# Last expert's result rows placed by a product on TensorE, the other rows gathered during that expert, and its up projection in two halves

## The chip, the core and the metric

The kernel runs on one core of a Trainium2 chip. The metric is the device time of one execution in microseconds (us), median of three runs. TensorE is called PE below, VectorE is DVE, ScalarE is ACT, GpSimd is POOL and SyncE is SP.

## What is computed

A two-layer decoder trunk on 512 tokens of 1024 values. Each layer adds a mixer's output to x, then the output of a mixture of 16 experts, of which every token uses two. The part that matters here is the second one, of both layers:

```
combine = jnp.einsum('tk,tke->te', top_w, jax.nn.one_hot(eid, N_EXPERTS)) * pg[:, None]
out = jnp.zeros_like(t)
for e in range(N_EXPERTS):
    y = (jax.nn.silu(t @ w_gate[e]) * (t @ w_up[e])) @ w_down[e]
    out = out + combine[:, e:e + 1] * y
```

Weights are float32: `w_gate[e]` and `w_up[e]` are 1024x512, `w_down[e]` is 512x1024. Behind layer 0 stands layer 1's norm and a convolution mixer, behind layer 1 the final norm.

## The kernel before

**Experts.** Only the tokens that picked an expert are computed, up to 96 (`CAP`) of them; a branch that these inputs do not take handles more. POOL gathers an expert's token rows from HBM (L557, into `xg`), PE turns them (L1887), ACT and DVE make a high and a low part of the turned rows (`xgT`), and each product is three matmuls of such parts (`mm3`, L1558 to L1560). Weights stream through a ring in SBUF (SP, L304), and ACT and DVE split them too, chunk by chunk of 128x1024: ACT casts the high part (L605), DVE subtracts for the low part (L911). The split ring has six chunks, so chunk c is split only when PE is done with chunk c-6 (`chunk_done`). One expert is 12 chunks: 4 gate, 4 up, 4 down.

**Order.** It is written out by hand. In step e PE does gate(e), turns the hidden rows of e-1 (L1911), up(e), turns the token rows of e+1, and down(e-1), 24 matmuls for each of the three projections. ACT does silu (L788), DVE the product silu*up (`hidden`, L1384, into `act_h`), both the copies of turned rows (ACT L793, DVE L1377) and of the result y (ACT columns 0 to 511, L801; DVE the rest, L1391), which ACT's queue then stores to HBM (L806). Steps 5 to 14 run in a loop; the last step has gate(15), turn, up(15), down(14), then alone turn of hidden(15) and down(15).

**Tail of a layer.** In `result_rows` DVE works out the weights of a token's two experts and the HBM rows of its two results (22 small instructions, L1338 to L1356), behind down(14). POOL waits until all 16 results are stored, and gathers them by tokens in eight DMAs of 128 rows (L572, two for each of four tiles of 128 tokens, into `y_back`). DVE adds them to x with their weights (`combine`, L1329, two instructions a tile). Then comes the norm: sum of squares on ACT (L648), root on POOL (L490, L493), scaling on DVE (L932). Behind layer 0 PE turns the tiles (L1540), ACT and DVE copy them (L639, L939), and PE starts the odd layer's projection in `first_piece`, for 256 tokens, when tiles 0 and 1 are copied. Behind layer 1 the scaled tiles are stored as the output (SP, L366).

## Time and profile before

| | us |
|---|---|
| median of three runs | 1208.0 (1206.04 to 1209.63) |
| the profiled execution, its own time | 1209.83 |
| its span in the trace | 1207.9 |
| PE busy | 1097.2 (91%) |
| DVE busy | 887.1 (73%) |
| ACT busy | 645.2 (53%) |
| POOL busy | 121.7 (10%) |

The span is the time from the first to the last recorded instruction. Busy shares are averages over stages; idle time on an engine counts only where the chain of waits goes through it. The granted clock is the share of 2.4 GHz that PE had; 0.5 is 1.2 GHz.

### The profile page before, as it was taken

The page shows a single profiled execution, that of the slowest core. Times are in us where ns is not written, and L with a number is a line of the kernel's source. Part 1 is how long each engine was busy: PE and PEld are TensorE (multiplying, and loading weights), DVE is VectorE, ACT ScalarE, POOL GpSimd, SP SyncE. Part 2 cuts the span into 40 slices and gives each one's busy share as a digit, 9 for nine tenths or more (in the row PEclk, how much of TensorE's full clock was granted, in tenths as well). Part 3 has the DMA queues.
Part 4 walks back from the last instruction along what each step waited for, and adds up shares of the span by engine and source line. Part 5 has one row for each costly group of instructions (what it writes and reads, how often), then busy time and mean ns, then how long its engine had stood idle before and what let it go on. Part 6 is the DMA issues. An engine that isn't in the chain of part 4 may idle for free.

```text
span 1207.9 us, 15260 instructions
## 1 busy us (share of the span) xinstructions
PE 1097.2 (91%) x5316; PEld 831.7 (69%) x5316; DVE 887.1 (73%) x1125; ACT 645.2 (53%) x799; POOL 121.7 (10%) x158
## 2 busy tenths in 40 slices
PE   5999999789899999999983899999999999999980
PEld 4776776567777777777762888778877777777750
DVE  5253555867788999999994462553688999999975
ACT  5133434421347888888871321232267888888841
POOL 2000000021211000000004100000111000000005
PEclk9998999889979999999996899999879999999995
DMA  8632222220259999999974633233169999999935
GB/s 302 189 125 70 79 79 70 70 88 13 75 190 356 378 408 396 397 397 411 410 283 158 255 106 104 70 105 105 71 224 359 402 391 396 410 397 396 418 123 208
DMA packets 77598, 286.35 MB, mean 237 GB/s; under 512 B 16647, under 2 KB 16647, under 8 KB 61164
## 3 DMA queue, kind: packets, MB, share of 16 engines
q1 hardware_dynamic: 65212, 241.64, 52.6%
q0 software_dynamic: 8608, 30.95, 7.9%
q10 hardware_dynamic: 3728, 13.11, 2.8%
q8 instruction: 30, 0.49, 0.2%
q14 instruction: 20, 0.16, 0.0%
HBM read 266.79 MB, written 20.20 MB: 238 GB/s over the span
## 4 chain that ended last, share of the span: by engine, by line
PE 83%; DVE 9%; ACT 2%; DMA 2%; issue 2%; POOL 1%; ACTq 0%; POOLq 0%; SPq 0%; DVEq 0%; PEldq 0%
PE ps L1558 25%; PE ps L1560 25%; PE ps L1559 24%; PE ps L1887 2%; DVE w_split L911 2%; PE ps L1540 1%; ACT w_split L605 1%; PE ps L1803 1%; DVE arena L1277 1%; DMA arena<-y_rows_dram,arena 1%; PE ps L1645 1%; DVE arena L932 1%; DVE x_sb L1329 1%; PE ps L1911 1%; DVE arena L1105 1%
## 5 line engine op out<-in xcount | busy, mean ns | idle before, releaser
L911 DVE TENSOR_TENSOR w_split<-ring,w_split 128x1024 fp32r<-128x1024 f32 x452 | 540.9, 1220 | 87.5 <-ACT w_split L605 75.4
L605 ACT CAST w_split<-ring 128x1024 fp32r<-128x1024 f32 x452 | 472.2, 1051 | 195.1 <-PE ps L1560 191.5
L1558 PE MATMUL ps<-w_split,hT 128*96 128x512 f32 (+1 forms) x960 | 391.4, 408 | 14.2 <-DVE hT L1377 6.2
L1560 PE MATMUL ps<-w_split,hT 128*96 128x512 f32 (+1 forms) x960 | 383.8, 400 | 0.0
L1559 PE MATMUL ps<-w_split,hT 128*96 128x512 f32 (+1 forms) x960 | 383.6, 400 | 0.0
L1558 PEld LDWEIGHTS ps<-w_split,hT 128*96 128x96 f32 (+1 forms) x960 | 165.0, 172 | 79.3 <-issue 11.6
L1560 PEld LDWEIGHTS ps<-w_split,hT 128*96 128x96 f32 (+1 forms) x960 | 164.1, 171 | 63.4
L1559 PEld LDWEIGHTS ps<-w_split,hT 128*96 128x96 f32 (+1 forms) x960 | 165.4, 172 | 57.5 <-issue 0.3
L1558 PE MATMUL ps<-hT,w_split 128*128 128x512 f32 (+1 forms) x384 | 147.5, 384 | 5.7 <-issue 4.1
L1559 PE MATMUL ps<-hT,w_split 128*128 128x512 f32 (+1 forms) x384 | 145.0, 378 | 0.0
L1560 PE MATMUL ps<-hT,w_split 128*128 128x512 f32 (+1 forms) x384 | 144.8, 377 | 0.0
L1558 PEld LDWEIGHTS ps<-hT,w_split 128*128 128x128 f32 x384 | 73.9, 193 | 26.6 <-issue 11.5
L557 POOL DMA_INDIRECT arena<-h_rows_dram,arena x30 | 42.3, 1410 | 435.4 <-PE ps L1887 356.4
L1560 PEld LDWEIGHTS ps<-hT,w_split 128*128 128x128 f32 x384 | 74.0, 193 | 13.3
L1559 PEld LDWEIGHTS ps<-hT,w_split 128*128 128x128 f32 x384 | 74.1, 193 | 12.3
L648 ACT ACTIVATE arena<-x_sb 128x1024 f32<-128x1024 f32 x20 | 21.2, 1058 | 84.1 <-DVE x_sb L1190 40.9
L490 POOL TENSOR_SCALAR st<-st 128x1 f32<-128x1 f32 (+1 forms) x28 | 15.5, 553 | 373.5 <-ACT arena L648 229.1
L1540 PE MATMUL ps<-ident,arena 128*128 128x128 f32 x128 | 20.8, 316 | 31.0 <-DVE arena L932 30.3
L932 DVE SCALAR_TENSOR_TENSOR arena<-x_sb,st,arena 128x1024 f32<-128x1024 f32 x20 | 31.8, 1588 | 23.1 <-POOL st L493 23.1
L702 ACT ACTIVATE x_sb<-x_sb,st 128x128 f32<-128x128 f32 (+3 forms) x32 | 17.8, 556 | 43.8 <-DVE st L1043 43.8
L1540 PEld LDWEIGHTS ps<-ident,arena 128*128 128x128 f32 x128 | 17.2, 164 | 34.3 <-DVE arena L932 22.8
L1038 DVE SCALAR_TENSOR_TENSOR x_sb<-ps,arena 128x256 f32<-128x256 f32 (+3 forms) x16 | 13.2, 823 | 37.4 <-PE ps L1645 37.4
(218 smaller groups left out, 846.4 us busy)
## 6 DMA issues: line engine op xcount, KB each, us to landing
ring<-in_exp_w_gate SPq DMA_DIRECT2D x64, 1024.0 KB, 10.5
ring<-in_exp_w_up SPq DMA_DIRECT2D x64, 1024.0 KB, 10.7
ring<-in_exp_w_down SPq DMA_DIRECT2D x64, 1024.0 KB, 11.7
ring<-in_w_in_even SPq DMA_DIRECT2D x14, 1024.0 KB, 10.1
y_rows_dram<-arena ACTq DMA_DIRECT2D x32, 384.0 KB, 6.9
ring<-in_w_in_odd SPq DMA_DIRECT2D x12, 1024.0 KB, 7.3
ring<-in_w_out_even SPq DMA_DIRECT2D x4, 1024.0 KB, 4.8
h_rows_dram<-arena POOLq DMA_DIRECT2D x8, 512.0 KB, 4.5
```

Of the source, the lines that this page charges most:

```text
L490: g.tensor_scalar(dst, src, 1.0 / width, EPS, ALU.mult, ALU.add).then_inc(pool_step, 1)
L557: g.indirect_dma_start(out=xg[0:CAP, e % 2, :], out_offset=None, in_=h_dram, in_offset=bass.IndirectOffsetOnAxis(ap=slot_tok[0:CAP, e:e + ...
L605: s.copy(hi_of(c), raw(c)).then_inc(hi_ready, 1)
L648: s.activation(junk, x_sb[:, t, :], ACT.Square, accum_out=st[:, t:t + 1]).then_inc(sumsq_ready, 1)
L702: s.activation(e_maps[:, u % 2, m, 0:n], e_maps[:, u % 2, m, 0:n], ACT.Exp, bias=st[:, 16 + c:17 + c], accum_out=st[:, 20 + c:21 + c]).the ...
L911: v.tensor_tensor(lo_of(c), raw(c), hi_of(c).bitcast(F32), ALU.subtract).then_inc(lo_ready, 1)
L932: ins = v.scalar_tensor_tensor(out=h_row, in0=row, scalar=st[:, 4 + t:5 + t], in1=gains, op0=ALU.mult, op1=ALU.mult)
L1540: last = nc.tensor.transpose(ps[:, turn_bank(n, t) + b, k * P:(k + 1) * P], h_rows[:, t, c * P:(c + 1) * P], ident[:, :])
L1558: mm(out, a[0], b[0], start=start, stop=False)
L1559: mm(out, a[1], b[0], start=False, stop=False)
L1560: return mm(out, a[0], b[1], start=False, stop=stop)
L1887: last = nc.tensor.transpose(ps[:, 5 + k // 4, (k % 4) * P:(k % 4) * P + CAP], xg[0:CAP, u, k * P:(k + 1) * P], ident[0:CAP, 0:CAP])
```

## The change

It changes both layers in the same way, from expert 13 on.

- **Order of the last expert.** The hidden rows of expert 14 are turned in the middle of down(13), and down(14) comes before gate(15), in PSUM banks 5 and 6. SP loads the weights in that order. y of 13, 14 and 15 is copied by ACT alone, in two copies each.
- **Halves.** up(15) is made as two products of 256 columns (24 matmuls each); the hidden rows of the first half are made and turned while the second is computed, and down(15) starts with them.
- **Gather.** POOL no longer waits for the store of expert 15; it gathers when experts 0 to 14 are stored. A token whose result is in expert 15's row gets the row of its other expert instead, with weight 0 in `combine`.
- **Product.** Four small fp16 products turn the last expert's 0/1 selection to `selT`; when y of 15 is in SBUF, eight plain float32 products of 128x512 (`last_rows`, K=96) put its rows at their tokens in all eight PSUM banks, and `add_last` adds them to x with weight `last_w`, one DVE instruction a tile.
- **Small work.** The row numbers (`result_rows`, now 16 instructions) are worked out before gate(15)'s splits; the weights (`result_weights`, 8 instructions) within down(15). The constants get an `ident16` (one memset and one select on POOL at the start). Two more steps (13, 14) are written out instead of looped.
- **Behind layer 0** DVE splits three of the four first chunks of the odd weights behind the adds.

The core of the diff:

```diff
@@ gpsimd, take_back
-                    for u in range(2):
-                        pool.wait_ge(y_stored[u], 16 * (E // 2) * (l + 1))
+                    pool.wait_ge(y_stored[0], 16 * (E // 2) * (l + 1))
+                    pool.wait_ge(y_stored[1], 16 * ((E // 2) * (l + 1) - 1))
+                    pool.wait_ge(last_sel_ready, l + 1)
@@ scalar, after step 14
+            def last_experts(l, n, c):
+                copy_last_y(1, 2, c, 16 * ((n - 2) // 2))
+                store_y(E - 3, n - 2, 1)
+                splits(c + 9)
+                copy_last_y(0, 5, c + 4, 16 * ((n - 1) // 2))
+                store_y(E - 2, n - 1, 0)
+                act.wait_ge(last_sel_turned, l + 1)
+                s.copy(selT[0:CAP, :, :], ps[0:CAP, 7, :].rearrange("p (t n) -> p t n", t=TT)).then_inc(last_sel_ready, 1)
+                splits(c + 13)
+                silu(n, c + 8)
+                splits(c + 14)
+                copy_last_actT(l, n, 0)
+                splits(c + 16)
+                copy_last_actT(l, n, 1)
+                splits(c + 18)
+                copy_last_y(1, 2, c + 16, 16 * (n // 2))
+                store_y(E - 1, n, 1)
@@ vector, after step 14
                 result_rows(l)
+                splits(c + 14)
+                last_hidden(l, n, c, 0)
+                splits(c + 15)
+                copy_last_actT(l, n, 0)
+                splits(c + 16)
+                last_hidden(l, n, c, 1)
+                result_weights(l)
+                copy_last_actT(l, n, 1)
@@ vector, behind layer 0
             experts(0)
-            splits(PIECE * (ODD_BASE + 1))
             combine(0, 0)
             combine(0, 1)
+            splits(PIECE * ODD_BASE + 1)
+            add_last(0, 0, x_ready)
+            add_last(0, 1, x_ready)
+            add_last(0, 2, x_freed)
             scaled(2, 0)
+            add_last(0, 3, x_freed)
             scaled(2, 1)
             low_part(2, 0)
-            combine(0, 2)
+            splits(PIECE * ODD_BASE + 4)
             low_part(2, 1)
-            combine(0, 3)
+            combine(0, 2, x_ready)
+            combine(0, 3, x_ready)
@@ tensor, after step 14
+            def last_expert(l, n, c):
+                down(n - 1, 0, c, None, bank=5)
+                ... (four products of sel and ident16)
+                gate(n, 1, c + 4, None)
+                for half in range(2):
+                    for k in range(KD):
+                        if half and k == KD // 2:
+                            pe.wait_ge(half_act, l + 1)
+                            turn_half(n, 0)
+                        last = mm3(ps[0:CAP, (1, 7)[half], 0:256], ..., slice(half * 256, half * 256 + 256), ...)
+                pe.wait_ge(half_actT, l + 1)
+                down_rows(1, c + 12, None, 0, 2)
+                pe.wait_ge(act_ready, n + 1)
+                turn_half(n, 1)
+                down_rows(1, c + 12, None, 1, 2)
+                pe.wait_ge(actT_ready, n + 1)
+                down_rows(1, c + 12, None, 2, 2)
+                down_rows(1, c + 12, None, 3, 2)
+            def last_rows(l):
+                for t in range(TT):
+                    for half in range(2):
+                        last = mm(ps[:, 2 * t + half, :], selT[0:CAP, t, :].bitcast(F32), y_sb[0:CAP, 1, half * 512:half * 512 + 512], ...)
+                    last.then_inc(last_full, 1)
```

DVE in the last expert of layer 1. Before, from the product silu*up of 15 to the row numbers:

```order
L1384 TENSOR_TENSOR arena<-arena,ps 96x512 [waits chunk_done,silu_ready]
L911 TENSOR_TENSOR w_split<-ring,w_split 128x1024 [waits hi_ready] x2
L1391 COPY arena<-ps 96x512 [waits y_stored0,chunk_done]
L1377 TENSOR_TENSOR hT<-ps,hT 128x4x96 [waits actT_hi]
L1338 TENSOR_REDUCE arena<-arena 128x4 [waits route_exp]
```

Now, from the end of the row numbers on (L1473 is the half product, L1483 the low part of turned hidden rows, L964 a weight chunk's low part):

```order
L1421 CAST arena<-arena 128x8 [waits dve_step]
L964 TENSOR_TENSOR w_split<-ring,w_split 128x1024 [waits hi_ready] x8
L1473 TENSOR_TENSOR arena<-arena,ps 96x256 [waits up_half,silu_ready]
L964 TENSOR_TENSOR w_split<-ring,w_split 128x1024 [waits hi_ready]
L1483 TENSOR_TENSOR hT<-ps,hT 128x2x96 [waits half_hi]
L964 TENSOR_TENSOR w_split<-ring,w_split 128x1024 [waits hi_ready]
L1473 TENSOR_TENSOR arena<-arena,ps 96x256 [waits chunk_done,silu_ready]
```

The row numbers now stand in front of eight splits, and a split stands in front of each half's low part.

ACT in the last expert of layer 1, before, from the last split but one to the store of 15 (L801 is half of y, L806 the store):

```order
L605 CAST w_split<-ring 128x1024 [waits chunk_done,slot_landed3] x2
L801 COPY arena<-ps 96x512 [waits y_stored0,chunk_done]
L806 DMA y_rows_dram<-arena 96x1024 [waits y_dve,y_act]
L793 CAST hT<-ps 128x4x96 [waits act_turned]
L801 COPY arena<-ps 96x512 [waits y_stored1,chunk_done]
L806 DMA y_rows_dram<-arena 96x1024 [waits y_dve,y_act]
```

Now, from the last split in front of y of 14 to the first half's turned rows (L824 and L825 are the halves of y, L860 the store, L846 `selT`, L834 half of the turned hidden rows):

```order
L622 CAST w_split<-ring 128x1024 [waits chunk_done,slot_landed0]
L824 COPY arena<-ps 96x512 [waits y_stored0,chunk_done]
L825 COPY arena<-ps 96x512
L860 DMA y_rows_dram<-arena 96x1024 [waits y_half1,y_half0]
L846 CAST hT<-ps 96x512 [waits last_sel_turned]
L622 CAST w_split<-ring 128x1024 [waits chunk_done,slot_landed0]
L622 CAST w_split<-ring 128x1024 [waits chunk_done,slot_landed1] x2
L622 CAST w_split<-ring 128x1024 [waits chunk_done,slot_landed2]
L805 ACTIVATE arena<-ps 96x512 [waits act_ready,chunk_done]
L622 CAST w_split<-ring 128x1024 [waits chunk_done,slot_landed2]
L834 CAST hT<-ps 128x2x96 [waits half_turned]
```

The store of 14 has moved in front of the silu of 15 and of the splits for up(15) and down(15); the turned rows of a half stand where those of the whole stood.

DVE behind layer 1's experts, before:

```order
L1329 SCALAR_TENSOR_TENSOR x_sb<-arena,x_sb 128x1024 [waits y_back_loaded0]
L1329 SCALAR_TENSOR_TENSOR x_sb<-arena,x_sb 128x1024 [waits dve_step]
L1329 SCALAR_TENSOR_TENSOR x_sb<-arena,x_sb 128x1024 [waits y_back_loaded1]
L1329 SCALAR_TENSOR_TENSOR x_sb<-arena,x_sb 128x1024 [waits dve_step]
L932 SCALAR_TENSOR_TENSOR arena<-x_sb,st,arena 128x1024 [waits norm_rstd,gain_loaded]
```

Now (L1393 is `combine`, L1381 `add_last`, L985 the scaling):

```order
L1393 SCALAR_TENSOR_TENSOR x_sb<-arena,x_sb 128x1024 [waits y_back_loaded0]
L1393 SCALAR_TENSOR_TENSOR x_sb<-arena,x_sb 128x1024 [waits dve_step]
L1393 SCALAR_TENSOR_TENSOR x_sb<-arena,x_sb 128x1024 [waits y_back_loaded1,dve_step]
L1393 SCALAR_TENSOR_TENSOR x_sb<-arena,x_sb 128x1024 [waits dve_step]
L1381 SCALAR_TENSOR_TENSOR x_sb<-ps,arena,x_sb 128x1024 [waits last_full,dve_step]
L1393 SCALAR_TENSOR_TENSOR x_sb<-arena,x_sb 128x1024 [waits y_back_loaded2]
L1393 SCALAR_TENSOR_TENSOR x_sb<-arena,x_sb 128x1024 [waits dve_step]
L1381 SCALAR_TENSOR_TENSOR x_sb<-ps,arena,x_sb 128x1024 [waits last_full,dve_step]
L985 SCALAR_TENSOR_TENSOR arena<-x_sb,st,arena 128x1024 [waits norm_rstd,gain_loaded]
```

Each tile has a third instruction, which waits for PE's product instead of for a DMA.

## Rows read from the trace of the kernel before

**Rows 1.** Waits: engine, line waited for, us in total, times, longest

```profile
POOL arena L572 <- DMA y_rows_dram<-arena: 75.9, 2, 39.3
PE ps L1540 <- DVE arena L932: 30.3, 4, 20.1
DVE x_sb L1329 <- DMA arena<-y_rows_dram,arena: 19.1, 4, 11.2
```

**Rows 2.** Windows: us, busy (instructions) by engine, clock, DMA share, GB/s

```profile
1136.40:1153.90 17.50, 17.50 (x85) 12.51 (x84) 16.65 (x17) 14.34 (x17) 0.57 (x1) 1.00 1.02 415
1173.80:1207.90 34.10, 0.00 (x0) 0.00 (x0) 15.84 (x13) 5.15 (x9) 16.04 (x16) 0.56 0.54 196
632.80:641.40 8.60, 8.52 (x24) 5.43 (x24) 4.36 (x23) 0.05 (x1) 0.00 (x0) 0.65 0.07 23
641.40:661.40 20.00, 0.00 (x0) 0.00 (x0) 9.47 (x8) 4.82 (x7) 11.92 (x11) 0.61 0.66 229
```

**Rows 3.** Chain of waits behind layer 1's down(15): start, us, what

```profile
1171.66 0.23 PE ps L1558
...
1173.83 0.70 DVE arena L1391
1174.60 3.70 DMA y_rows_dram<-arena
1178.34 0.75 issue
...
1180.38 5.33 DMA arena<-y_rows_dram,arena
1185.73 1.30 DVE x_sb L1329
...
1201.98 1.28 DVE arena L932
```

**Rows 4.** Timeline of layer 0's tail: start, us, engine, line, instruction, idle before

```profile
653.61 2.61 DVE L1329 SCALAR_TENSOR_TENSOR x_sb<-arena,x_sb 128x1024 f32<-128x1024 f32 x2 [6.62 <-DMA arena<-y_rows_dram,arena]
...
660.09 1.29 DVE L932 SCALAR_TENSOR_TENSOR arena<-x_sb,st,arena 128x1024 f32<-128x1024 f32 x1 [0.54 <-POOL st L493]
...
668.14 1.22 DVE L939 TENSOR_TENSOR hT<-ps,hT 128x1024 fp32r<-128x1024 f32 x1
...
669.46 0.55 PE L1558 MATMUL ps<-hT,w_split 128*128 128x256 f32 x1 [4.05 <-issue]
```

**Rows 5.** Timeline, DVE: product silu*up of three experts; splits, low parts

```profile
625.02 0.68 DVE L1384 TENSOR_TENSOR arena<-arena,ps 96x512 f32<-96x512 f32 x1
...
1143.25 0.68 DVE L1384 TENSOR_TENSOR arena<-arena,ps 96x512 f32<-96x512 f32 x1
1143.85 0.95 DVE L1370 TENSOR_TENSOR hT<-ps,hT 128x768 fp32r<-128x768 f32 x1
1144.71 4.81 DVE L911 TENSOR_TENSOR w_split<-ring,w_split 128x1024 fp32r<-128x1024 f32 x4
...
1160.88 0.68 DVE L1384 TENSOR_TENSOR arena<-arena,ps 96x512 f32<-96x512 f32 x1
```

**Rows 6.** Timeline of layer 1's last expert: ACT's casts, PE, copies, small instructions

```profile
1158.39 0.39 PE L1558 MATMUL ps<-w_split,hT 128*96 128x512 f32 x1
...
1164.12 0.58 ACT L801 COPY arena<-ps 96x512 f32<-96x512 f32 x1 [1.66 <-PE ps L1560]
...
1166.25 0.16 DVE L1338 TENSOR_REDUCE arena<-arena 128x4 f32<-128x16 f32 x1
1166.39 0.47 PE L1558 MATMUL ps<-w_split,hT 128*96 128x512 f32 x1 [1.98 <-DVE hT L1377]
...
1168.25 0.63 PE L1559 MATMUL ps<-w_split,hT 128*96 128x512 f32 x1
...
1171.31 0.17 DVE L1356 CAST arena<-arena 128x8 int32<-128x8 f32 x1
```

**Rows 7.** POOL's gathers: timeline of two of experts, one of L572; L557's durations

```profile
430.32 0.92 POOL L557 DMA_INDIRECT arena<-h_rows_dram,arena  x1 [16.66 <-PE ps L1887]
448.39 1.70 POOL L557 DMA_INDIRECT arena<-h_rows_dram,arena  x1 [17.15 <-PE ps L1887]
1181.63 0.94 POOL L572 DMA_INDIRECT arena<-y_rows_dram,arena  x1 [0.30 <-issue]
L557 POOL DMA_INDIRECT arena<-h_rows_dram,arena x30: 907/914/4657, 347.8 to 1106.8; - x30
```

**Rows 8.** PE: float32 products of 1280 columns; first of two of 256 columns

```profile
269.37 2.32 PE L1691 MATMUL ps<-arena 128*128 128x512 f32 x8
673.10 0.28 PE L1560 MATMUL ps<-hT,w_split 128*128 128x256 f32 x1
673.22 0.28 PE L1558 MATMUL ps<-hT,w_split 128*128 128x256 f32 x1
```

264 lines of the change are left out of this document (188 added, 76 removed).

## Prediction

> **What bounds the kernel now.** I read the table of waits first. PE works 91% of the span, so its long holes are what can be had. The longest wait of PE is 20.1 us for a scaled tile, and the largest wait for a DMA is POOL's, twice, for the stored results [rows 1]. Next the windows: in an expert PE is busy all the time at full clock (17.5 of 17.5 us) with DVE at 16.65, so the experts are bound by PE with DVE close behind; in the two tails PE does nothing for 34.1 us (layer 1) and 20.0 us (layer 0) [rows 2]. The chain of waits shows of what the tail is made in layer 1: down(15) ends at 1173.75 (call this T), y is copied, the store takes 3.70 us, POOL starts 0.75 us later, the first pair of gathers has landed at 1185.7, then DVE adds and scales to 1203.3, and the output's store ends the span at 1207.9 [rows 3]. Layer 0 has the same until PE starts `first_piece` at 669.46, when tiles 0 and 1 are copied [rows 4]; T is 641.3 there, the end of the window of down(15) [rows 2]. Last, down(15) itself: PE waits 1.98 us for its turned rows in layer 1, and then runs some matmuls at the lower clock, 0.43 us apart in place of 0.23 (8 of them, 1.6 us) [rows 3, 6]. In layer 0 the window's clock is 0.65 and the 24 matmuls take 8.5 us in place of 5.5 [rows 2].
>
> **The sum, first part: when does down(15) end?** I lay the new order on layer 1's times; layer 0 is the same 535.86 us earlier (1160.88 and 625.02) [rows 5]. Steps repeat every 17.6 us (1143.25 to 1160.88), so down(13) starts at 1140.8, one step before 1158.39 [rows 5, 6].
>
> - Its middle (12 matmuls, 2.76 us) is at 1143.6, but the product of 14 ends at 1143.93: 0.5 us of wait, 0.5 for four turns, and down(13) ends at 1147.3.
> - DVE does the product, the copy of 0.95, two splits (1.22 each) and the low part of 14 (0.55) by 1147.7 [rows 5]. So down(14) runs from 1147.8 to 1153.3, four small fp16 products add 0.4, gate(15) runs from 1153.7 to 1159.2.
> - DVE meanwhile: two splits to 1150.1, then 16 small instructions. Before, 22 took 5.2 us [rows 6], so 3.8 us, to 1153.9. Eight splits at 1.22 take it to 1163.7. PE wants the last chunk of up(15) at 1161.3, which DVE has at 1161.2: no wait there, but no slack either.
> - Matmuls of 256 columns are 0.12 us apart [rows 8], so the halves cost 48 x 0.12 = 5.7 us against 5.5. The first half ends at 1162.1, the middle of the second is at 1163.5; DVE's half product (half of 0.68, 0.4) is there at 1164.1: 0.6 us of wait.
> - Then a row of five: turn 0.3, ACT's copy 0.3, ACT's cast of the next chunk 1.05, DVE's split 1.22 and its low part 0.4, to 1167.5. PE was done with the second half at 1165.8: 1.8 us of wait. This is the wait that takes the place of the 1.98.
> - Row 0 of down(15) 1.4 us, second half product and turn (wait 0.6), row 1, then DVE's 8 small instructions and low part (wait 0.4), rows 2 and 3: T = 1174.1. I add the 1.6 us of low clock that the old wait of this size cost: **T = 1175.7**, 2 us later than before.
>
> In layer 0 the same gives 639.8, 1.5 us earlier than 641.3: there the old order also held DVE for two more splits, and the clock was down longer.
>
> **Second part: the gathers.** ACT copies y of 14 in two pieces of 0.58 [rows 6] behind down(14), so the store goes at 1154.7. At 3.7 us and 0.75 POOL starts at 1159.2, during expert 15, 20 us before the old 1179.1. Eight gathers at a pitch of 1.24 (0.94 and 0.30) [rows 7], each pair landed 5.33 us behind its second issue [rows 3]: 1165.8, 1168.3, 1170.8, 1173.3. In layer 0 the weights still stream; with 2 to 3 us more the pairs are there from 633 to 641. DVE is not free before 1171.3 + 1.2 of clock + some 1.3 for its branch = 1173.8 (layer 0: 637.9). So the gathers are hidden, with 5 us to spare, and **DVE becomes the bound of the tail**.
>
> **Third part: DVE's tail in layer 1.** One add of 1024 elements takes 1.30, also from PSUM, as the low part with a PSUM operand shows (1.22) [rows 3, 4]. Tiles 0 and 1: 1173.8 to 1179.0. The float32 products: 1280 columns take 2.3 less 0.15 of latency, 1.7 ns a column [rows 8], so 0.87 us for each of eight, 7.0 us in all, behind T and two copies of y (1.3 us): from 1177.0, first tile full at 1178.8, the last at 1184. The first add ends at 1180.3; tile 2 and its neighbour's add and scaling follow at 2.6, 1.3 and 1.3. All in all DVE works 4 x 2.6 + 4 x 1.3 + 4 x 1.3 = 20.8 us with some 1.0 of waits for the root, from 1173.8 to 1195.6. The output needs 4.65 more as before (1203.26 to 1207.9): 1200.3. **Layer 1 gains 7.6 us.**
>
> **Layer 0.** Combine 0 and 1 from 637.9 to 643.1, one split, three adds to 648.3 (the third is full at 646.4 at full clock). The root comes 3.86 us behind the first add, as before (656.22 to 660.09) [rows 4], so tile 0 is scaled at 650.6, add 3 and tile 1 to 653.2, PE's turn and the copies to 655.1, three splits (3.7) and the low part (1.22): PE starts at 660.1 against 669.46. Combine 2 and 3 lie behind that, under the 7 us of `first_piece` that come before their tiles. **Layer 0 gains 9.3 us.** The weights behind it load when the gathers are done, so earlier. Behind 669 PE waits almost nowhere up to the next experts, so the gain is kept.
>
> **At nothing**: the store of y(15), 384 KB among landed gathers; `ident16` on POOL, which idles at the start; the fp16 copy `selT`, behind ACT's store with PE in gate(15).
>
> Sum: 7.6 + 9.3 = 16.9 us. The profiled execution took 1209.83 with a span of 1207.9; it lies 1.8 above the median, so 1192.9 for it and **1191** for the median.
>
> **A rule against it.** The gathers now run while DVE is busy. Those of the experts do so already: 914 ns is the median of 30, some take 1.70, one 4.66 [rows 7]. The Trainium skill says in "GPSIMD Engine Reference", section 1 "Specifications", that GpSimd's SBUF interfaces are shared with VectorE and that DVE instructions with two SBUF inputs, as all splits are, contend for them. By that rule every gather could be slow, by the rows most are not. At 1.70 (pitch 2.0) the last pair lands at 1179.3 where it is wanted at 1185.4, so nothing changes.
>
> **Rivals.**
>
> 1. **PE's clock stays low through the products.** Against it: PE's hole in front of them is 1.3 us, less than the 1.98 behind which PE had full clock at first. For it: waits of 0.5, 0.6, 1.8 and 0.6 come just before. At 1.2 GHz the eight take 13.9. In layer 1 the first two adds slip by 2 us; in layer 0 the third and fourth tile are full at 651.5 and 655, the scaling and the turn behind them slip, and PE starts at 664.8: 4.7. Together 6.7: **1198**. Half of that if the clock is low for part of them, 1194, which my range for the likeliest covers.
> 2. **DVE has no backlog.** If the small instructions go at 0.2 us and the clock holds through down(15), T is 1.6 to 2 us earlier in each layer and DVE free with it: **1187**.
> 3. **DVE is later than I have it.** Each us of backlog at gate(15) goes into T and DVE's tail both. With 2.5 us in each layer: **1196**. Slack is nil in my sum, which speaks for it.
> 4. **Slower: POOL starves under DVE.** If each gather took the 4.66 us of the slowest, a pair every 9.9 us: in layer 1 pairs land at 1173, 1183, 1193 and 1203, and behind the last come 2.6 of adds, 1.3 of the last expert's, 2.5 for the root, 1.3 and 4.65: 1215.4, 7.5 us later than before; in layer 0 the second pair lands at 650 where it is wanted at 640.5, and the gain is gone: **1215.5**. It decides from a pitch of 2.7 us on (the wanted times above), and the whole is slower than before from 4.1 on, since 8 and 4 us go with each us of pitch. Against it: the median of the 30 is 0.91.
> 5. **The gathers start late all the same** (a store that waits, a semaphore): then the old tail stands and four adds and the products come on top, 5 us a layer: 1218.
>
> **Chances.** The forecast with its neighbourhood (1188 to 1195) 0.58; rival 1 0.13; rival 2 0.12; rival 3 0.12; rival 4 0.03; rival 5 0.02. A time of 1186 to 1199 takes in the first three rivals but the outer part of each, 0.85 or so. This kernel can be told from no change at about 0.3%, 3.6 us. Faster by more: 0.94; within: 0.03; slower: 0.03.
>
> **What would show it.** First gather near 1159 less layer 0's gain, at the pitch of 1.24; the first combine of each tail without a wait for a DMA; PE's wait for the first half's low part 1.8 us; T 2 us later than before in layer 1 (in its own frame), 1.5 earlier in layer 0; `last_rows` 7.0 us; `first_piece` near 660; DVE working 21 of 22 us in the last tail. The prediction is wrong if DVE waits for `y_back` or for `last_full` by more than 2 us, or if PE stalls within gate(15) or up(15).

## The result: 1180.1 us against 1207.0

| | before | after |
|---|---|---|
| median of the timed runs | 1207.0 us (1205.0 to 1209.6, 4 runs) | **1180.1 us** (1179.9 to 1180.9, 4 runs) |
| ratio | | 0.9777, 95% interval 0.9756 to 0.9798 |
| span of the profiled execution | 1207.9 | 1178.3 |

The change gains 27 us. I had forecast 16.9, 1191 us with a range from 1186: the sign and the mechanism came out, the size did not, and the time lies below the range. The gain stands where it was looked for. Here are the waits of after that answer to [rows 1] (engine, line waited for, us in total, times, longest):

```profile
POOL arena L589 <- DMA y_rows_dram<-arena: 33.1, 2, 17.8
...
PE ps L1662 <- DVE arena L985: 12.3, 5, 9.7
...
PE ps L1680 <- DVE w_split L964: 4.1, 2, 2.4
```

GpSimd waits 33 us for stored results instead of 76, and the row of VectorE waiting for gathered rows (19.1 us in four) is gone. TensorE's wait of 20.1 us for a scaled tile in layer 0's tail is gone too: there its two waits for scaled tiles are now 0.85 and 1.30 us, and the 9.7 in the row above lies ahead of the experts, as it does in before. Of the 4.1 us that TensorE waits for splits, 1.7 are in layer 1's last expert and 2.4 ahead of the experts. TensorE is now busy 94% of the span. Next the windows that answer to [rows 2] (us, busy us of PE, PEld, DVE, ACT and POOL, granted clock, DMA share, GB/s): in layer 1 from within down(13) into up(15), then the end of up(15) with the wait and the last down projection, the products, the tail; then layer 0's last down projection and its tail up to `first_piece`:

```profile
1124.90:1142.50 17.60, 17.48 (x90) 12.65 (x89) 17.17 (x31) 15.30 (x19) 2.72 (x2) 1.00 0.76 293
1142.50:1154.50 12.00, 10.19 (x62) 7.66 (x60) 8.95 (x18) 2.56 (x5) 6.82 (x7) 1.00 0.89 307
1154.50:1163.00 8.50, 7.11 (x16) 2.96 (x16) 7.76 (x8) 2.29 (x5) 1.85 (x2) 1.00 0.28 99
1163.00:1178.30 15.30, 0.00 (x0) 0.00 (x0) 9.69 (x8) 3.35 (x6) 4.25 (x6) 0.60 0.34 138
628.00:634.80 6.80, 6.16 (x26) 3.86 (x26) 5.72 (x15) 2.21 (x3) 3.81 (x4) 1.00 0.94 338
634.80:652.10 17.30, 9.29 (x33) 4.69 (x33) 17.15 (x16) 7.39 (x10) 2.56 (x4) 0.95 0.90 325
```

What to see is the clock: 1.00 through both last down projections and the products, where before had 0.65 in layer 0's. And in layer 0's tail VectorE is busy 17.15 of 17.3 us, where it had 9.47 of 20.0.

The chain around layer 1's last down projection, from the timeline (start, us, engine, line, instruction, idle before and what ended it). L1682 at 1146.25 ends up(15), L1680 at 1148.21 is row 0 of the last down projection and at 1151.42 its row 2, L1483 is the low part of a turned half, L1393 is `combine`, L1381 `add_last`, L985 `scaled`, L2103 `last_rows`:

```profile
1146.25 0.28 PE L1682 MATMUL ps<-w_split,hT 128*96 128x256 f32 x1
...
1148.21 0.44 PE L1680 MATMUL ps<-w_split,hT 128*96 128x512 f32 x1 [1.68 <-DVE w_split L964]
...
1151.01 0.36 DVE L1483 TENSOR_TENSOR hT<-ps,hT 128x192 fp32r<-128x192 f32 x1
1151.42 0.48 PE L1680 MATMUL ps<-w_split,hT 128*96 128x512 f32 x1
1151.90 5.25 DVE L1393 SCALAR_TENSOR_TENSOR x_sb<-arena,x_sb 128x1024 f32<-128x1024 f32 x4 [0.54 <-issue]
...
1154.04 0.40 PE L1682 MATMUL ps<-w_split,hT 128*96 128x512 f32 x1
1155.68 7.11 PE L2103 MATMUL ps<-arena,hT 96*128 96x512 f32 x16 [1.25 <-ACT arena L825]
1157.75 1.28 DVE L1381 SCALAR_TENSOR_TENSOR x_sb<-ps,arena,x_sb 128x1024 f32<-128x1024 f32 x1 [0.59 <-PE ps L2103]
...
1172.41 1.28 DVE L985 SCALAR_TENSOR_TENSOR arena<-x_sb,st,arena 128x1024 f32<-128x1024 f32 x1 [0.94 <-POOL st L509]
```

VectorE adds gathered rows 2.5 us ahead of the end of the down projection (T = 1154.44), where in before it began 12.0 us behind it [rows 3]. It waits 0.59 us for the product and 0.94 us for the last root. With the 0.54 us ahead of its first combine, that is all of VectorE's idle time in this tail.

**A ruler.** Whole executions of one kernel differ by some 6 us (before: 1203.3 to 1209.6), e3b's by 8. Much of the difference lies ahead of the tails. One place is the step from the product of expert 1 to that of expert 2: in the 28 layers of the 14 profiled executions it took 20.7 us twenty times and 19.1 eight times (in e1, e7, e10 and e11 in one of the two layers alone), with a granted clock of 0.82 in the first half of after's 20.7 and 1.00 in e7's 19.1. So I read each trace also by three marks: H, the start of the product silu*up of expert 14 (in each layer), and F, the start of `first_piece`. Tail 0 is F less H, tail 1 is the end of the span less the second H; what lies between F and the second H took 470.5 to 473.8 us, without regard to the change.

| kernel | median us | tail 0 | tail 1 | both, against after |
|---|---|---|---|---|
| before | 1207.0 | 62.1 | 64.7 | +26.5 |
| after | 1180.1 | 46.8 | 53.4 | 0 |
| e1 gathers late | 1208.9 | 61.7 | 67.4 | +28.8 |
| e2 products twice | 1189.1 | 53.0 | 55.1 | +7.9 |
| e3 before, 80 fillers | 1206.2 | 61.2 | 64.9 | +25.9 |
| e3b before, 91 fillers | 1205.1 | 60.6 | 63.1 | +23.5 |
| e4 weights early | 1179.5 | 47.2 | 53.2 | +0.2 |
| e5 order | 1179.7 | 45.9 | 53.2 | -1.1 |
| e6 weights last | 1179.8 | 47.5 | 52.8 | +0.1 |
| e7 rows early | 1177.6 | 45.6 | 51.7 | -2.9 |
| e8 whole up | 1186.4 | 49.1 | 55.6 | +4.4 |
| e11 whole up, filled | 1180.8 | 47.5 | 54.1 | +1.4 |
| e10 tail order | **1176.3** | 45.1 | 50.2 | -5.0 |

The last column is rounded after the subtraction. A tail comes from one profiled execution, a median from 4 to 12 timed ones. Two executions of the same code differ by 1.6 us in one tail (tail 1 of before and of e3b), so a smaller difference in the tails counts only where rows show what it is made of. After has four executions within 1.0 us, but e4's five spread from 1176.5 to 1181.9; medians closer than some 3 us are not told apart by themselves.

### The profile page after: what moved, and what is told of

It reads as the page before. It is cut to its first block, busy times and chain, and to the rows that moved or that the text cites. A ratio compares the mean times of both kernels' runs of the same rounds, so it can differ in the third digit from the quotient of the medians.

```text
span 1178.3 us, 15323 instructions
## 1 busy us (share of the span) xinstructions
PE 1105.9 (94%) x5404; PEld 835.9 (71%) x5404; DVE 891.4 (76%) x1133; ACT 648.6 (55%) x809; POOL 119.0 (10%) x160
## 4 chain that ended last, share of the span: by engine, by line
PE 83%; DVE 10%; ACT 3%; issue 2%; DMA 1%; POOL 1%; POOLq 0%; SPq 0%; ACTq 0%; DVEq 0%; PEldq 0%
PE ps L1680 25%; PE ps L1682 24%; PE ps L1681 24%; DVE w_split L964 2%; PE ps L2009 1%; ACT w_split L622 1%; DVE arena L985 1%; DVE arena L1330 1%; PE ps L1767 1%; PE ps L1925 1%; DVE arena L1158 1%; PE ps L1662 1%; PE ps L2033 1%; PE ps L1881 1%; PE ps L1946 1%
## 5 line engine op out<-in xcount | busy, mean ns | idle before, releaser
L964 DVE TENSOR_TENSOR w_split<-ring,w_split 128x1024 fp32r<-128x1024 f32 x452 | 540.3, 1221 | 87.4 <-ACT w_split L622 75.4
L1680 PE MATMUL ps<-w_split,hT 128*96 128x512 f32 (+2 forms) x976 | 391.2, 401 | 11.1 <-DVE w_split L964 4.1
L1681 PE MATMUL ps<-w_split,hT 128*96 128x512 f32 (+2 forms) x976 | 383.8, 393 | 0.0
L1682 PE MATMUL ps<-w_split,hT 128*96 128x512 f32 (+2 forms) x976 | 383.7, 393 | 0.0
L1680 PEld LDWEIGHTS ps<-w_split,hT 128*96 128x96 f32 (+1 forms) x976 | 165.8, 170 | 75.3 <-issue 14.7
L1682 PEld LDWEIGHTS ps<-w_split,hT 128*96 128x96 f32 (+1 forms) x976 | 165.5, 170 | 61.4
L1680 PE MATMUL ps<-hT,w_split 128*128 128x512 f32 (+1 forms) x384 | 147.4, 384 | 6.4 <-issue 4.6
L1682 PE MATMUL ps<-hT,w_split 128*128 128x512 f32 (+1 forms) x384 | 144.7, 377 | 0.0
L1680 PEld LDWEIGHTS ps<-hT,w_split 128*128 128x128 f32 x384 | 74.2, 193 | 27.0 <-issue 12.2
L1682 PEld LDWEIGHTS ps<-hT,w_split 128*128 128x128 f32 x384 | 74.0, 193 | 13.0
L985 DVE SCALAR_TENSOR_TENSOR arena<-x_sb,st,arena 128x1024 f32<-128x1024 f32 x20 | 31.7, 1587 | 21.1 <-POOL st L509 21.1
L1449 DVE TENSOR_TENSOR hT<-ps,hT 128x768 fp32r<-128x768 f32 x30 | 28.4, 948 | 0.4 <-ACT hT L798 0.3
```

The lines of the kernel that those rows point to most:

```text
L964: v.tensor_tensor(lo_of(c), raw(c), hi_of(c).bitcast(F32), ALU.subtract).then_inc(lo_ready, 1)
L985: ins = v.scalar_tensor_tensor(out=h_row, in0=row, scalar=st[:, 4 + t:5 + t], in1=gains, op0=ALU.mult, op1=ALU.mult)
L1449: v.tensor_tensor(xgT[:, u, 1, :, 0:CAP], ps[:, 5:7, :].rearrange("p b (k c) -> p (b k) c", k=4)[:, :, 0:CAP], xgT[:, u, 0, :, 0:CAP].bitc ...
L1680: mm(out, a[0], b[0], start=start, stop=False)
L1681: mm(out, a[1], b[0], start=False, stop=False)
L1682: return mm(out, a[0], b[1], start=False, stop=stop)
```

## Experiments on what was gained

**e1: the gathers wait for the last store again.**

```diff
-                    pool.wait_ge(y_stored[1], 16 * ((E // 2) * (l + 1) - 1))
+                    pool.wait_ge(y_stored[1], 16 * (E // 2) * (l + 1))
```

> GpSimd waits for the store of expert 15 too before it gathers; the product on TensorE, the halves and every order stay. In the kernel before, the first pair of rows had landed 12.0 us behind the end of the last down projection (1173.75 to 1185.73). Theory A (the gain is the gathers' overlap): VectorE's first combine starts 12 us behind that end instead of 2.5 us ahead of it, so each layer loses about 14.3 us, in layer 0 up to 3 us more if TensorE's clock then falls in the longer wait: 1180.1 + 28.6 = 1209 us, range 1206 to 1213, no faster than before. Theory B (the earlier end of the last down projection and the shorter chain of weights carry a good part, the gathers are hidden in part anyway): half of that, 1195 us or less.

Measured: 1208.9 us, ratio to before 1.0023 (1.0010 to 1.0036). Theory A (1208.7 before rounding). The first combine in layer 1:

```profile
1178.57 2.60 DVE L1393 SCALAR_TENSOR_TENSOR x_sb<-arena,x_sb 128x1024 f32<-128x1024 f32 x2 [14.74 <-DMA arena<-y_rows_dram,arena]
```

So the change is worth nothing, or slightly less, without the early gathers; the product, the halves and the moved down projections do not pay by themselves. This run is also rival 5 of the prediction, the gathers late all the same: it was priced at 1218 and came to 1208.9. In layer 0 the 16 turns ran at 1.97 us for eight in place of 1.09, behind TensorE's wait of 15.1 us: first add 14.2 us later than after's, `first_piece` 14.8 later. The low clock costs that tail 0.7 us, not more.

**e2: each product made twice.** In `last_rows` the pair of products of a tile is issued two times over.

> After with each of the 16 products of the last expert's rows made twice (7.1 us of TensorE more in each layer). The prediction took the product as a term on the way of 1.25 + 1.8 us only up to the first add, the rest hidden under VectorE's combines. Layer 1: product pairs ready at 1159.2, 1162.8, 1166.3, 1169.9 for adds that stood at 1157.8, 1161.6, 1166.6 and 1168.9: 1.5 to 2 us. Layer 0: the turns wait until TensorE has finished at 650.3 and not 644.0: 6 to 7 us. Theory A (so hidden): 1180.1 + 1.8 + 6.4 = 1188.3 us, range 1187 to 1190. Theory B (it is on the path with its full length): 1194. Theory C (layer 0's turns are not what its tail waits for): 1184 or less.

Measured: 1189.1 us (0.9862, 0.9843 to 0.9882), +9.0 against after (tails +7.9: 6.2 in layer 0, 1.7 in layer 1). Theory A. In layer 1 most of the added 7.1 us lies under VectorE's adds; in layer 0 the turns of the next norm stand behind the products on TensorE, so there it is hidden only while TensorE is free by 644.

## Experiments on what the forecast missed

The forecast took the low clock of before's layer 1 (1.6 us in the last down projection [rows 3, 6]) into both layers of after. It did not come. Is it the halves that kept it away?

**e8: the up projection of expert 15 in one piece.**

```diff
-                for half in range(2):
-                    for k in range(KD):
...
+                gate_or_up(1, 1, c + 8, None)
+                turn_act(n)
                 pe.wait_ge(y_half0, n - 1)
                 pe.wait_ge(y_half1, n - 1)
...
                 pe.wait_ge(actT_ready, n + 1)
...
+                for k in range(KF):
+                    down_rows(1, c + 12, None, k, 2)
```

with VectorE's and ScalarE's splits up to c + 16 ahead of one product, one copy and one low part.

> After with expert 15's up projection made in one piece of 512 columns, turned and split in one piece, VectorE's and ScalarE's splits ahead of the product; the weights stay behind the product. Theory A (the halves save little, since TensorE waits 1.68 us with them for VectorE's and ScalarE's order): TensorE waits product 0.6, turn 0.5, ScalarE's copy 0.5, and VectorE's weights and copy to 2.6 us behind the up projection's end, and then runs 5.6 us without a stop: end of the last down projection 0.3 us later than after's, 1180.7 us, range 1180 to 1181.7. Theory B (the halves are worth the 2.5 us by which the wait shrank from 4.24 to 1.68): 1185 us. If a wait of that length also pulls TensorE's clock down, as the prediction assumed from the kernel before (granted 0.61 to 0.65 there), 1.6 us more in each layer in either theory.

**e11: e8 with TensorE kept busy in its two waits.**

```diff
                 gate_or_up(1, 1, c + 8, None)
+                for _ in range(3):
+                    mm(ps[:, 7, :], ones16[:, :], later[:, 0:1].broadcast_to([P, 512]), start=True, stop=True)
                 turn_act(n)
+                for _ in range(6):
+                    mm(ps[:, 7, :], ones16[:, :], later[:, 0:1].broadcast_to([P, 512]), start=True, stop=True)
```

> e8_whole_up with fp16 matmuls of 512 columns on ones, into a bank that nobody reads, in TensorE's two waits behind the whole up projection (three ahead of the turn, six behind it, 0.22 us each). In e8_whole_up the first rows of the last down projection ran at 0.43 us a matmul for 3.4 us in layer 0 (8 of them) and 3.1 us in layer 1 and then at 0.23; each layer lost 3.1 us to after. Theory A (half of that loss is TensorE's clock, which falls in those waits): all rows at 0.23, 1.5 us less in each layer than e8_whole_up's 1186.4: 1183.4 us, range 1182.5 to 1184.3, and the loss that stays is the wait itself. Theory B (the slow rows come from something else that falls together with the wait, such as the gathers' traffic, busy there too): rows still at 0.43, 1186.4, range 1185.7 to 1187.2.

Measured: e8 1186.4 us (ratio to before 0.9827, 0.9814 to 0.9841), e11 1180.8 (0.9790, 0.9776 to 0.9803). The timeline of TensorE in e8, layer 1, behind the last matmul of up at 1150.82: turn, first rows of the last down projection:

```profile
1152.06 0.55 PE L2027 MATMUL ps<-ident,arena 96*128 96x96 f32 x4 [0.85 <-DVE arena L1461]
...
1154.22 0.71 PE L1674 MATMUL ps<-w_split,hT 128*96 128x512 f32 x1 [1.61 <-DVE hT L1454]
1154.73 0.63 PE L1675 MATMUL ps<-w_split,hT 128*96 128x512 f32 x1
1155.16 0.63 PE L1676 MATMUL ps<-w_split,hT 128*96 128x512 f32 x1
...
1157.29 0.48 PE L1675 MATMUL ps<-w_split,hT 128*96 128x512 f32 x1
1157.61 0.39 PE L1676 MATMUL ps<-w_split,hT 128*96 128x512 f32 x1
```

and in e11:

```profile
1147.43 1.47 PE L2072 MATMUL ps<-later,ones 128*128 128x512 f16 x6
...
1149.20 0.44 PE L1674 MATMUL ps<-w_split,hT 128*96 128x512 f32 x1 [0.30 <-DVE hT L1454]
```

In e8 the matmuls of 512 columns come 0.43 us apart after two waits of 0.85 and 1.61 us (a turn between them), until 1157.3, at a granted clock of 0.52 (1154.2 to 1157.6); that is the 1.2 GHz level against 0.23 us apart at 2.4 GHz. In e11 the gathers and the DMA traffic are still there (DMA share 0.92 from 1146 to 1155), TensorE is busy, and no row is slow. By the tails the clock is worth 1.6 us in layer 0 (49.1 less 47.5) and 1.5 in layer 1; the medians say 5.5 together, more than the tails' 3.1, and their spreads allow both. What the halves save in waits alone is the rest: 0.6 and 0.7 us. **So the halves' own worth is mostly that their single wait of 1.68 us does not lower the clock**, and theory A of e11 holds in its mechanism; its time, 1183.4 with a range from 1182.5, was 2.6 us too high, which is within what one median can be off. Theory B of e8 named about the right time (1185) for the wrong reason; A with its clause on the clock gives 1183.9, against 1184.5 by the tails and 1186.4 by the median.

**e3 and e3b: the kernel before with TensorE kept busy in layer 0's tail.** The same filler, 80 and 91 times, behind `experts(0)`.

> The kernel before with 80 fp16 matmuls of 512 columns on ones, written to a bank nobody reads, behind layer 0's last down projection, so that TensorE is busy through most of the 20 us in which it waited. Theory A (the low clock is a price that before paid in layer 0's tail and after does not): the 16 turns at 661.4, 3.97 us at granted clock 0.50, take about 2.2, and the first products behind them (clock 0.84 over 669.5 to 680) about 1.5 us less: the whole is 3 us below before, 1204 us, range 1202 to 1205.5. Theory B (the clock there is hidden by VectorE's and ScalarE's copies between the turns and the products): within 0.7 us of before, 1207. If the filler outlasts the wait it costs what it outlasts: turns later than 661.4 would show that.

> The kernel before with 91 in place of 80 filler matmuls behind layer 0's last down projection. With 80 the filler ended at 658.6, TensorE then waited 2.67 us, the second eight turns ran at 1.97 us again, and the first products began 1.1 us earlier than in before. With 91 it ends near 661.0 and the 16 turns should all run at full clock (1.10 us for eight), the first products 1.9 us earlier than in before and at full clock from the start. Theory A (the low clock costs before about 1.1 to 2 us in this tail): 1205.1 us, range 1204.3 to 1206. Theory B (nothing, VectorE is late in any case): 1206.7, range 1206.2 to 1207.3.

Measured: 1206.2 us (ratio 0.9998, 0.9987 to 1.0009) and 1205.1 (0.9989, 0.9979 to 1.0000). With 91 both turns are fast:

```profile
636.64 19.99 PE L1999 MATMUL ps<-later,ones 128*128 128x512 f16 x91
656.75 1.10 PE L1540 MATMUL ps<-ident,arena 128*128 128x128 f32 x8
658.75 1.09 PE L1540 MATMUL ps<-ident,arena 128*128 128x128 f32 x8 [0.91 <-DVE arena L932]
663.90 0.55 PE L1558 MATMUL ps<-hT,w_split 128*128 128x256 f32 x1 [4.05 <-issue]
```

From the end of the last down projection to `first_piece` it takes 27.3 (e3) and 27.1 us (e3b), against 28.1 in before. I had expected 3 us of e3 and got 1 in this tail; its median is what theory B said and can't be told from before. Turns are short, and VectorE's and GpSimd's work on the second tile stands between them. e3b falls in its theory A by the median (1205.1, 1.3 below before) and short of it in that tail (1.0 us instead of 1.9). The rest of its profiled gain was an accident that says more. In e3b's layer 1 nothing was changed, and the row behind the wait of 1.98 us is this:

```profile
1157.55 0.48 PE L1558 MATMUL ps<-w_split,hT 128*96 128x512 f32 x1 [1.98 <-DVE hT L1377]
```

All its matmuls run 0.23 us apart (granted clock 1.00 from 1157.3 to 1162.8, against 0.68 from 1166.3 to 1171.7 in before), and tail 1 is 63.1 instead of 64.7. In e3's layer 1, behind the same wait, eight matmuls are slow as in before. **The same wait lowers the clock in one execution and not in another.** The step from expert 1 to 2 is a second place of this kind, 1.6 us at a time. Behind the halves' wait, on the other hand, the clock held in every profiled case: 1.68 us in both layers of after, e1 and e2, 1.75 in both of e4, eight in all. The prediction took its 1.6 us from one execution.

**e9: GpSimd beside VectorE, measured by itself.** Behind the end of after, six stretches like this one, with another VectorE instruction in each:

```diff
+            for p in range(6):
...
+                for k in range(6):
+                    pool.wait_ge(last_sel_turned, 2 + 8 * p + k + 1)
+                    g.tensor_scalar(bench[:, 0:1], bench[:, 0:1], 0.5, 0.25, ALU.mult, ALU.add).then_inc(last_sel_turned, 1)
+                for k in range(2):
+                    g.indirect_dma_start(out=y_back[:, 3, k, :], out_offset=None, in_=y_dram[0:(E - 1) * CAP, :],
+                                         in_offset=bass.IndirectOffsetOnAxis(ap=back_idx[:, k:k + 1], axis=0)
+                                         ).then_inc(v_copied, 16)
...
```

> After, with a piece of work behind its end that measures GpSimd beside VectorE: six times, GpSimd runs six small multiplications of 128 numbers and issues two row gathers, while VectorE runs in turn nothing, an addition of two SBUF tensors, of a PSUM and an SBUF tensor, a scaling of one SBUF tensor, a copy of SBUF, a copy of PSUM (12 instructions of 128x1024 each). The output is that of after; the time is longer by the added work, some 90 us. Theory A (GpSimd stands still while VectorE reads two SBUF tensors, and at no other time): small ones about 1.2 us in the second stretch and 0.2 in all others; gathers' issues 1.9 and over there and 0.94 elsewhere. Theory B (it is slowed by any SBUF traffic of VectorE): slow in four or five of the six stretches. Theory C (fast copies on SBUF alone hold it up too): slow in the stretches of two SBUF tensors, of the scaling and of the SBUF copy.

Measured: 1249.7 us in the one execution made, 70 longer than after. GpSimd's timeline, beside an addition of two SBUF tensors, of PSUM and SBUF, a scaling of an SBUF tensor, a copy of SBUF, a copy of PSUM:

```profile
1181.91 7.06 POOL L616 TENSOR_SCALAR bench<-bench 128x1 f32<-128x1 f32 x6
1189.12 1.90 POOL L618 DMA_INDIRECT arena<-y_rows_dram,arena  x1
1191.33 0.94 POOL L618 DMA_INDIRECT arena<-y_rows_dram,arena  x1 [0.30 <-issue]
...
1197.44 1.56 POOL L616 TENSOR_SCALAR bench<-bench 128x1 f32<-128x1 f32 x6
...
1208.91 4.30 POOL L616 TENSOR_SCALAR bench<-bench 128x1 f32<-128x1 f32 x6
...
1221.52 4.30 POOL L616 TENSOR_SCALAR bench<-bench 128x1 f32<-128x1 f32 x6
...
1232.76 1.55 POOL L616 TENSOR_SCALAR bench<-bench 128x1 f32<-128x1 f32 x6
```

and one VectorE instruction of the first and of the third kind:

```profile
1177.62 1.22 DVE L1672 TENSOR_TENSOR arena<-arena 128x1024 f32<-128x1024 f32 x1
...
1208.10 0.69 DVE L1676 TENSOR_SCALAR arena<-arena 128x1024 f32<-128x1024 f32 x1
```

An instruction on 128 numbers takes GpSimd 1.18 us, the pace of VectorE's additions, beside two SBUF inputs, 0.72 beside a fast SBUF-only scaling or copy (those take 0.69), and 0.26 where one operand is in PSUM. That is theory C for the small instructions. It fits that the scaling starts 3.86 us behind an add in before, where a combine of two SBUF tensors runs beside the root, while in after's layer 0, where `add_last` reads PSUM, the root is ready 2.1 us behind the add.

Of the gathers this run says less: beside the same additions one issue took 1.90 us and the next 0.94, beside the scaling they took 1.38 and 1.15, and elsewhere 0.94 to 0.97. The gathers of the experts in before [rows 7] were not as harmless as the prediction read them: of 30, 22 took 0.91 to 1.19 us, four 1.70, two 2.6 and two, not one, 4.66. The 4.66 us come at the same place in both layers of after too, between the products of experts 1 and 2, where VectorE copies and then makes four splits in a row; in e7, where four small instructions come first, that gather takes 0.91. In e5, e6, e7 and e10 one gather of a tail took 2.5 to 3.4 us beside two splits. Why the twelve additions in a row of this run did not do the same stays open.

The Trainium skill says in "GPSIMD Engine Reference", section 1 "Specifications", that the SBUF interfaces are shared, with contention with VectorE instructions in a 2-port perf mode or with two SBUF inputs. This run agrees for the small instructions beside two SBUF inputs (1.18 us) and beside a PSUM operand (0.26). That the scaling and the copy of SBUF alone ran in such a mode is my reading of their 0.69 us, against 1.22 for an addition of as many elements.

## Experiments on what sets the tail, and a faster version

**e4: the weights in VectorE's wait for ScalarE.**

```diff
                 last_hidden(l, n, c, 0)
+                result_weights(l)
                 splits(c + 15)
                 copy_last_actT(l, n, 0)
                 splits(c + 16)
                 last_hidden(l, n, c, 1)
-                result_weights(l)
                 copy_last_actT(l, n, 1)
```

> After, with the nine small VectorE instructions of the weights (1.65 us, 1149.33 to 1150.98 in layer 1) moved up into the 2.24 us in which VectorE waits for ScalarE at 1144.2. Theory A (VectorE's row of work sets the tail): each layer gains 1.6 us, 1176.9 us. Theory B (the product's end sets it: the first add already waited 0.59 us for it, and TensorE waited only 0.23 us at 1151.2 for what stands behind the weights): VectorE's first combine comes 1.6 us earlier and the first add waits 2 us; each layer gains 0.2 to 0.6, 1179.3 us, range 1178.8 to 1179.9.

Measured: 1179.5 us (0.9773, 0.9750 to 0.9796), tails +0.2. The five executions spread too far to tell the theories apart by the median; the tails say theory B: VectorE's row of work and the product are both late by the same; taking 1.65 us from one of them gives next to nothing.

**e5 and e6: the second half's product ahead of the last splits.** e5 has the order hidden 0, weights, low part 0, hidden 1, two splits, low part 1; e6 the same with the weights at the end.

> The weights as in the run with them early, and VectorE copies the first half's operand and multiplies the second half ahead of the two splits that it now makes after: TensorE should start the last down projection's row 0 at 1146.5 and not at 1148.21. Theory A and B of that run agree here: end of the last down projection 1.6 us earlier and VectorE free 1.6 us earlier, so 1.6 to 1.8 us in each layer, 1176.7 us, range 1176 to 1177.6. Rival: rows 2 and 3 then wait for their splits and their operand (split c+16 ends at 1149.3, operand 1149.7, row 2 due at 1149.8), which if each takes 0.3 us longer gives back 0.5 a layer: 1177.7.

> The order of e5_order, with the nine small VectorE instructions of the weights behind everything else of the expert. In e5_order VectorE and ScalarE went on 0.9 to 1.6 us after the records of TensorE's last matmul before their wait, against 0.04 us elsewhere. Theory A (that lag came with the burst of short instructions just ahead of the wait): the second half's product starts at the end of the up projection, the last down projection ends 1.6 us before after's and the first combine no later than in after; the first add then waits for the combines and not for the product: 1179.0 us, range 1178.3 to 1179.7. Theory B (it comes with starting the down projection's row 0 right behind the up projection, whatever VectorE did): the lag is there again, the end of the last down projection no earlier than in after, 1180.1, range 1179.7 to 1181.

Measured: 1179.7 us (0.9776, 0.9759 to 0.9792) and 1179.8 (0.9772, 0.9759 to 0.9786). e5 missed its 1176.7 by 3 us, and e6 came out 0.1 above its theory A's range. In both TensorE starts row 0 without a wait. In e5 (layer 1) VectorE's product of the second half should start with up's end at 1148.46:

```profile
1148.18 0.28 PE L1682 MATMUL ps<-w_split,hT 128*96 128x256 f32 x1
...
1150.10 0.42 DVE L1473 TENSOR_TENSOR arena<-arena,ps 96x256 f32<-96x256 f32 x1 [2.19 <-PE ps L1682]
...
1152.24 0.32 ACT L834 CAST hT<-ps 128x192 fp32r<-128x192 f32 x1 [2.94 <-PE ps L2060]
```

It starts 1.6 us after it, and ScalarE's copy 1.3 us after the turn it waits for. In e6:

```profile
1148.40 0.28 PE L1682 MATMUL ps<-w_split,hT 128*96 128x256 f32 x1
...
1148.79 0.42 DVE L1473 TENSOR_TENSOR arena<-arena,ps 96x256 f32<-96x256 f32 x1 [0.76 <-PE ps L1682]
1149.12 2.35 DVE L964 TENSOR_TENSOR w_split<-ring,w_split 128x1024 fp32r<-128x1024 f32 x2
...
1150.27 0.32 ACT L834 CAST hT<-ps 128x192 fp32r<-128x192 f32 x1 [0.74 <-PE ps L2060]
```

0.1 us and 0.04 us: theory A of e6 on the lag. The down projection then ends 1.8 us earlier, counted from up's end (6.1 us against 7.9), tail 1 is 0.6 us shorter as expected, but tail 0 is 0.6 longer: TensorE is done with the products earlier while the next norm is not, its hole grows from 0.85 to 2.46 us, and the turns fall to the low clock (1.97 us for eight, not 1.09). A gain on TensorE alone was given back as clock. Why the lag comes is open: ScalarE has it too, with no short instructions before it, and in e4's layer 0 ScalarE had one of 1.0 us.

**e7: VectorE's row numbers and weights spread over experts 1 to 4 and 13.** `result_rows` is cut in four parts, one behind each of experts 1 to 4, `result_weights` stands behind expert 13, and the last expert has e6's order.

> VectorE's row numbers (3.2 us) and weights (1.65 us) are spread in five pieces behind experts 1, 2, 3, 4 and 13, where TensorE sets the pace and VectorE is busy 95% of the time; in the last expert the order of e6_weights_last. Theory A (VectorE's slack of about 0.9 us an expert hides them, and the tail begins both with an earlier end of the last down projection and an earlier free VectorE): 1.6 us less in each layer, 1176.9 us, range 1176 to 1178. Theory B (each piece delays an operand that TensorE waits for in the steady part, and the gain is eaten there): 1179 to 1181, with new waits of TensorE for VectorE in experts 2 to 5.

Measured: 1177.6 us (0.9760, 0.9746 to 0.9775), tails -2.9. Theory A, whose range is 1176 to 1178: both chains become shorter, so it counts. The pieces cost next to nothing where they went: in layer 1 it is 231.9 us from the product of expert 1 to that of expert 14, against 231.6 in after, which the tails don't count. The executions (1174.8 to 1180.3) overlap those of after; the rows of the tails are what decides. Tail 1 shows what then bounds:

```profile
1145.92 5.23 DVE L1393 SCALAR_TENSOR_TENSOR x_sb<-arena,x_sb 128x1024 f32<-128x1024 f32 x4
1152.38 1.28 DVE L1381 SCALAR_TENSOR_TENSOR x_sb<-ps,arena,x_sb 128x1024 f32<-128x1024 f32 x1 [1.23 <-PE ps L2109]
```

**e10: e7 with VectorE's tail in another order.**

```diff
-            for t in range(TT):
-                combine(1, t)
...
+            for t in range(3):
+                combine(1, t)
+            add_last(1, 0, x_ready)
+            combine(1, 3)
+            add_last(1, 1, x_ready)
+            add_last(1, 2, x_ready)
+            scaled(4, 0)
+            add_last(1, 3, x_ready)
+            scaled(4, 1)
+            scaled(4, 2)
+            scaled(4, 3)
```

and in layer 0 the split of the odd stage's first piece between `combine(0, 0)` and `combine(0, 1)`.

> The best version that the runs point to: e7_rows_early with VectorE's tail written in another order. Layer 1: combines of tiles 0, 1, 2 ahead of the first add (VectorE waited 1.23 us for the product there), and the add of tile 3 three instructions ahead of its scaling (it waited 0.93 us for GpSimd's root); layer 0: the split of the odd stage's first piece between the first two tiles' combines, where VectorE waited 0.68 us for rows. Theory A (VectorE's waits go and nothing takes their place): layer 1 2.1 us, layer 0 0.7 us less, 1174.8 us, range 1174 to 1176. Theory B (the output's stores, which now leave later and closer together, or GpSimd's root beside VectorE's two-SBUF instructions take the place): no better than 1177.6, range 1176.6 to 1178.3.

Measured: **1176.3 us** (0.9753, 0.9741 to 0.9766), the fastest of all, 3.8 us below after, and no execution of it is as slow as after's fastest. It lies between the ranges of both theories. Tails -5.0, of which 2.0 beyond e7 and not 2.8: in layer 1 the wait of 1.23 is gone, but the root of the last tile still costs 0.72, its GpSimd instruction beside a scaling; in layer 0 the wait for rows is gone and waits of 0.30 and 0.43 for the products came:

```profile
638.38 1.28 DVE L1381 SCALAR_TENSOR_TENSOR x_sb<-ps,arena,x_sb 128x1024 f32<-128x1024 f32 x1 [0.30 <-PE ps L2111]
640.10 1.28 DVE L1381 SCALAR_TENSOR_TENSOR x_sb<-ps,arena,x_sb 128x1024 f32<-128x1024 f32 x1 [0.43 <-PE ps L2111]
...
1168.30 1.28 DVE L985 SCALAR_TENSOR_TENSOR arena<-x_sb,st,arena 128x1024 f32<-128x1024 f32 x1 [0.72 <-POOL st L509]
```

## Why the prediction was wrong in size

I lay after on before's times by H: 2.1 us are added in layer 0 and 18.34 in layer 1 (1143.25 less 1124.91).

- **The gathers.** Right. First one at 1157.8 in before's frame, forecast 1159.2; the issues took 0.94 us at a pitch of 1.24, but for the first two, which took 1.88 and 1.92 us beside splits, and one of 1.04; nobody waited for them. That VectorE becomes the bound of the tail is right too: the add of 1157.75 waited 0.59 us, no other combine or add waited. e1 shows that without this step nothing of the gain is left; e8 shows that 4.4 us of it (by the tails) also need the halves. The order with down(14) ahead of gate(15) was not tested by itself.
- **T, the end of the last down projection: the step that failed, 2.9 us in each layer.** Forecast 1175.7 and 639.8, measured 1172.8 and 636.9. Of this 1.6 is the term "the 1.6 us of low clock that the old wait of this size cost". The wait came, 1.68 us, the clock stayed. The term was not unreasonable (e8 pays it, after 0.85 and 1.61 us) but it was carried over as certain from one execution of another wait; e3b and the eight cases above show that it need not come. Rival 2 had it at nothing. The other 1.3 is mostly VectorE's backlog: row numbers 3.2 us where I had 3.8, splits at 1.17 instead of 1.22, so that neither the turn in the middle of down(13) nor the half product waited (0.5 and 0.6 forecast; up ended 0.9 us earlier), and 0.4 in the down projection, where TensorE lost 0.23 us at row 2.
- **Layer 0 behind T: 3.0 us more than forecast** (`first_piece` 17.3 us behind T, forecast 20.3). Root: I took the 3.86 us of before [rows 4], and it was ready 2.1 us behind the add, in time for a scaling at 2.4: 1.1 us on the path; e9 shows what sets it. Turn and copies: 1.9 us in the sum, and in fact 1.1, VectorE's low part of the first tile, which began without a wait because the turn took 1.09 us; where it took 1.97 (e1, e6) VectorE waited 0.72 us there: 0.8. VectorE free 0.4 earlier, against T, since its branch took 0.8 and not 1.3. The rest, 0.7, is small steps: adds and scalings come 1.2 us apart where I had 1.3, splits and low parts 1.14 where I had 1.22.
- **Layer 1 behind T: 0.7 us**, the branch (0.54, not 1.3). From the first combine to the end I had 26.5 us and it took 26.4.
- **The products.** 7.0 forecast, 7.11 measured, each layer at full clock. Rival 1 did not come. e2 confirms how they are hidden.

The sum: 2 x 2.9 + 3.0 + 0.7 = 9.5 us, and the forecast missed by 26.5 - 16.9 = 9.6. **Rival 2 (no backlog, the clock holds: 1187) was the nearest** and got a chance of 0.12. Its conditions came true, the small instructions at 0.20 us each and the clock at 1.00, but its price was still 7 us too high: it took 1.6 to 2 us off T where 2.9 were due, and nothing off the tails behind T. Of the 9.5 us, 4.0 are one mechanism, the clock (1.6 in each T and the 0.8 of layer 0's turn); the other 5.5 are many VectorE and GpSimd terms, all set too high, and a range that reached 5 us below the forecast did not hold both. The rival "slower, POOL starves" did not come in these tails: six of the eight gathers of layer 1 took 0.94 to 1.04 us and none held anybody up.

What stays open: whether the clock falls behind a wait is not decided by the wait's length alone (1.68 and 1.75 us behind the halves: no, in all eight cases; 1.98 in before: yes, in e3: yes, in e3b's layer 1: no; 0.85 and 1.61 in e8: yes in both layers), and the lag of e5.

## What to carry to other kernels

When a wait of TensorE goes or shrinks, count what the clock did behind it as a second, uncertain term with both its values, and put it in the range for all its places at once; keeping the engine busy with matmuls on nothing (e11) tells the two apart in one run. When two chains end within a few tenths of a us of each other, shortening one gives nothing (e4, e6) and both together give most of what was expected (e7: 2.9 of 3.2 us): look for work that can go where another engine sets the pace. And write small GpSimd work so that it runs beside VectorE instructions that read PSUM.

## What the runs showed of the hardware

- GpSimd's instruction on 128 numbers: 0.26 us beside VectorE reading PSUM, 0.72 beside SBUF-only scaling or copies, 1.18 beside two SBUF inputs (e9). The issue of a row gather takes 0.94 us, and 1.9 at times beside two SBUF inputs (e9); one in e5's layer 0, beside splits, took 3.37, and one beside four splits in a row 4.66 (both layers of before and after).
- The lower level costs TensorE's last down projection 1.5 to 1.6 us in before's layer 1 and in e8 (8 matmuls 0.43 us apart in place of 0.23), and more behind before's wait of 4.24 us in layer 0 (14 of them); behind the wait of 1.98 us the same code ran at either level in different executions.
- VectorE and ScalarE resumed 0.6 to 1.6 us after the end of what they waited for in e5 (both layers), against 0.04 to 0.1 us in e6. Not explained.
- The eight float32 products of 512 columns take 7.11 us, 0.89 us each or 1.7 ns a column; the trace shows each as two records of 0.44 us.
